# A one-core decoder kernel: the layer norms' statistics, transposes and evacuations rearranged by token halves

## What is computed

```python
for i in range(DEPTH):                      # DEPTH = 4
    kind, j = i % N_MIXERS, i // N_MIXERS   # fox, s5, pool, fox
    ...                                     # m = the mixer of h
    h = layer_norm(DN_ALPHA * h + m, ln_g[i, 0], ln_b[i, 0])
    h = layer_norm(DN_ALPHA * h + swiglu(h, ffn_w1[i], ffn_w3[i], ffn_w2[i]), ln_g[i, 1], ln_b[i, 1])

def layer_norm(h, g, b):
    mu = jnp.mean(h32, axis=-1, keepdims=True)
    var = jnp.mean(jnp.square(h32 - mu), axis=-1, keepdims=True)
    return ((h32 - mu) * lax.rsqrt(var + LN_EPS) * g + b).astype(h.dtype)
```

## Time and profile before

| | |
|---|---|
| median of the three runs | 1341.6 us (1338.08 to 1341.9) |
| the profiled execution, its own time | 1344.52 us |
| its span, first to last instruction | 1342.4 us |
| PE busy | 1247.0 us (93%) |
| DVE busy | 858.6 us (64%) |
| ACT busy | 606.3 us (45%) |
| granted TensorE clock, mean | 0.936 of 2.4 GHz |

### The profile page before, as it was taken

One profiled execution on the slowest core, in us unless ns is written; L12 is line 12 of the kernel. 1 busy time (PEld: TensorE's weight loads), 2 busy tenths in 40 slices (PEclk: granted clock), 3 DMA queues, 4 the chain that ended last, 5 costly groups with the idle time before them and its releaser, 6 DMA issues.

```text
span 1342.4 us, 20829 instructions
## 1 busy us (share of the span) xinstructions
PE 1247.0 (93%) x8432; PEld 1114.0 (83%) x8432; DVE 858.6 (64%) x1291; ACT 606.3 (45%) x944; POOL 160.2 (12%) x206
## 2 busy tenths in 40 slices
PE   5998899989989998999997789999989988999996
PEld 3886799989978766999996769999968976999996
DVE  5775879999575445655557866555567765655556
ACT  4465454444443224444444445444454653544442
POOL 2530008930090000000000000000002000000000
PEclk9997899989986778999998899999999988999998
DMA  9442356445585332665562536655535322566651
GB/s 356 157 150 78 110 189 204 142 154 188 162 187 164 129 111 95 225 198 188 188 189 98 170 110 196 218 184 188 186 127 188 118 88 94 189 220 188 187 184 69
DMA packets 63377, 220.35 MB, mean 164 GB/s; under 512 B 7985, under 2 KB 9777, under 8 KB 62513
## 3 DMA queue, kind: packets, MB, share of 16 engines
q1 hardware_dynamic: 56914, 202.50, 46.4%
q0 software_dynamic: 5504, 14.95, 3.8%
q10 hardware_dynamic: 864, 1.57, 0.4%
HBM read 210.34 MB, written 7.60 MB: 162 GB/s over the span
## 4 chain that ended last, share of the span: by engine, by line
PE 77%; DVE 15%; issue 3%; ACT 2%; DMA 1%; SPq 0%; DVEq 0%; ACTq 0%
PE bank L1249 15%; PE bank L1251 14%; PE bank L1250 14%; PE bank L1260 8%; PE bank L1262 8%; PE bank L1264 8%; DVE wlo L750 3%; PE bank L1274 2%; PE bank L1493 2%; DVE xlo L817 1%; DVE stats L763 1%; DVE slot L762 1%; PE bank L1424 1%; PE bank L1437 1%; ACT whi L462 1%
## 5 line engine op out<-in xcount | busy, mean ns | idle before, releaser
L750 DVE TENSOR_TENSOR wlo<-raw,whi 128x1024 fp32r<-128x1024 f32 x370 | 460.0, 1247 | 111.5 <-ACT whi L462 111.3
L1249 PE MATMUL bank<-xhi,whi 128*128 128x256 f32 x1728 | 498.7, 289 | 14.9 <-DVE xlo L817 10.1
L1250 PE MATMUL bank<-xlo,whi 128*128 128x256 f32 x1728 | 493.9, 286 | 0.0
L1251 PE MATMUL bank<-xhi,wlo 128*128 128x256 f32 x1728 | 493.7, 286 | 0.0
L462 ACT ACTIVATE whi<-raw 128x1024 fp32r<-128x1024 f32 x370 | 387.8, 1053 | 143.4 <-PE bank L1264 128.9
L1249 PEld LDWEIGHTS bank<-xhi,whi 128*128 128x128 f32 x1728 | 336.3, 195 | 24.2 <-DVE wlo L750 13.7
L1250 PEld LDWEIGHTS bank<-xlo,whi 128*128 128x128 f32 x1728 | 336.9, 195 | 2.8
L1251 PEld LDWEIGHTS bank<-xhi,wlo 128*128 128x128 f32 x1728 | 336.5, 195 | 0.0
L854 DVE TENSOR_TENSOR hval<-bank,silu 128x256 f32<-128x256 f32 x88 | 37.3, 424 | 231.0 <-PE bank L1251 231.0
L510 ACT ACTIVATE hhi<-hval 128x256 fp32r<-128x256 f32 x84 | 35.1, 418 | 194.3 <-DVE hval L854 194.3
L1260 PE MATMUL bank<-whi,hhi 128*128 128x512 f32 x304 | 95.3, 395 | 1.8 <-DVE wlo L750 1.8
(11 more groups left out here) (289 smaller groups left out, 1483.2 us busy)
## 6 DMA issues: line engine op xcount, KB each, us to landing
raw<-in_w SPq DMA_DIRECT2D x370, 512.0 KB, 3.9
slot<-in_ln_row POOLq DMA_DIRECT2D x16, 512.0 KB, 5.7
toep<-slot POOLq DMA_DIRECT2D x8, 512.0 KB, 15.3
toepA<-toep SPq DMA_DIRECT2D x2, 1024.0 KB, 7.4
BT<-toep SPq DMA_DIRECT2D x2, 1024.0 KB, 4.9
x_tm<-in_x SPq DMA_DIRECT2D x1, 1024.0 KB, 5.0
slot<-in_s_B SPq DMA_DIRECT2D x1, 1024.0 KB, 10.9
slot<-in_s_C SPq DMA_DIRECT2D x1, 1024.0 KB, 14.1
```

The source lines that it names most:

```text
L750: V.tensor_tensor(wlo[:, c % SPL, :], raw[:, c % RAW, :], whi[:, c % SPL, :].bitcast(F32), ALU.subtract).then_inc(w_lo, 1)
L1249: mm(dst, wh, bhi[:, kc, :], start=(i == 0), stop=False)
L1250: mm(dst, wh, blo[:, kc, :], start=False, stop=False)
L1251: ins = mm(dst, wl, bhi[:, kc, :], start=False, stop=(i == len(chunks) - 1))
```

## The change

The change is in the norms and at their edges.

1. **First half's statistics.** The two residual additions of token half 0 also write their row sums (`accum_out=sums`); a 128x1 instruction makes the negative mean `nmean`; ACT squares `res + nmean` over all 1024 columns with a row sum (`ssq`) and takes the square root of that. The two `bn_stats` and the `bn_aggr` of half 0 are gone. Half 1 keeps them.
2. **Transposes to separate banks.** Half 0 goes to banks 0 and 1 (four chunks each), half 1 to banks 4 to 7 (two chunks each). Every pair of transposes signals.
3. **Evacuation half by half.** Each 128x256 scale-and-shift becomes two of 128x128, one for each half: of half 0, pairs 0 and 1 by ACT, 2 and 3 by DVE; of half 1, pairs 0 and 2 by DVE, 1 and 3 by ACT. `xhi` of pair 0 is made in two halves. The second half's norm on DVE is issued in two pieces of 512 columns.
4. **Weight tiles.** Tile `first` is split before the norm (in the tails of `ffn`, `fox` and `poolmix`). In the norm only `first + 1` is split: by ACT behind the norming of half 0, by DVE at the very end. Before, DVE split `first` in front of `xlo` of pair 0 and the tiles up to `ahead` in front of `xlo` of pairs 2 and 3.
5. **End of a sublayer.** In `tm_end` the first of the three tiles is finished on bank 3 before bank 2 is complete.

```diff
@@ residual, DVE
-                step(V.scalar_tensor_tensor(res[:, m, cols], x_tm[:, m, cols], ALPHA, src, ALU.mult, ALU.add))
-                return V.bn_stats(stats[:, m, j, :], res[:, m, cols])
+                if m == 0:
+                    mark(V.scalar_tensor_tensor(res[:, m, cols], x_tm[:, m, cols], ALPHA, src, ALU.mult, ALU.add, accum_out=sums[:, j:j + 1]))
+                else:
+                    step(V.scalar_tensor_tensor(res[:, m, cols], x_tm[:, m, cols], ALPHA, src, ALU.mult, ALU.add))
+
+            def measure(j):
+
+                mark(V.bn_stats(stats[:, j, :], res[:, 1, j * HALF:(j + 1) * HALF]))
@@ ln, DVE
+                    summed(0, 0)
+                    summed(0, 1)
+                    marked()
+                    V.tensor_scalar(nmean[:, :], sums[:, 0:1], sums[:, 1:2], -1.0 / D, ALU.add, ALU.mult).then_inc(mean_ready, 1)
+                    summed(1, 0)
+                    if glu is None:
+                        measure(0)
+                    if n < n_ln - 1:
+                        mean_rstd(n, 0)
+                        dve.wait_ge(mean_ready, n + 1)
+                        V.tensor_scalar(nmr[:, :], nmean[:, :], rstd[:, 0, :], None, ALU.mult).then_inc(rstd_ready, 1)
+                    summed(1, 1)
+                    if glu is not None:
+                        measure(0)
+                    measure(1)
+                    marked()
+                    V.bn_aggr(mv[:, :], stats[:, :, :]).then_inc(var_ready, 1)
...
+                    value(2, 0)
+                    dve.wait_ge(var_ready, n + 1)
+                    mean_rstd(n, 1)
+                    for j in range(2):
+                        cols = slice(j * HALF, (j + 1) * HALF)
+                        V.tensor_scalar(res[:, 1, cols], res[:, 1, cols], mv[:, 0:1], rstd[:, 1, :], ALU.subtract, ALU.mult).then_inc(xn_ready[1], 1)
...
+                value(3, 0)
+                value(0, 1)
+                x_lo(0)
+                value(2, 1)
+                x_lo(1)
+                x_lo(2)
+                x_lo(3)
+                lo_to(ahead if n < 0 else first + 1)
@@ ln, ACT
+                    act.wait_ge(mean_ready, n + 1)
+                    step(nc.scalar.activation(slot[4][:, 0:D], res[:, 0, :], ACT.Square, bias=nmean[:, :], accum_out=ssq[:, :]))
+                    nc.scalar.activation(std[:, 0, :], ssq[:, :], ACT.Sqrt, scale=1.0 / D, bias=cst[:, C_EPS:C_EPS + 1]).then_inc(std_ready, 1)
...
+                value(0, 0)
+                value(1, 0)
+                act.wait_ge(xval0_act, 2 * (n + 1) + 1)
+                high0(0)
+                act.wait_ge(xval1_dve, 2 * (n + 1) + 1)
+                high0(1).then_inc(xhi_ready, 1)
+                value(1, 1)
+                high(1)
+                high(2)
+                value(3, 1)
+                high(3)
@@ tails of ffn (ACT; DVE the same with lo_to), fox, poolmix
                 nxt[0] = T0 + T_FFN
+                hi_to(T0 + T_FFN)
...
-                for c in range(KC - 2):
+                for c in range(KC - 1):
                     hi_to(T0 + KC + 2 * PAIRS + c + 2)
@@ tm_end, PE
-                for i in range(3):
-                    ins = all3(i, 2)
-                ins.then_inc(sub_done, 1)
-                for i in range(3):
-                    used(all3(i, 3))
+                all3(0, 2)
+                used(all3(0, 3))
+                all3(1, 2)
+                all3(2, 2).then_inc(sub_done, 1)
+                used(all3(1, 3))
+                used(all3(2, 3))
@@ lnT, PE
+                        ins = nc.tensor.transpose(xn_at(m, 2 * b + q), src[:, m, (2 * b + q) * P:(2 * b + q + 1) * P], ident)
+                        ins.then_inc(xnT_ready, 1)
```

More of the change, by code:

```diff
@@ new lines, in ln, with value @@
+                else:
+                    hi_to(ahead)
+                def value(b, m):
+                    act.wait_ge(xnT_ready, 8 * (n + 1) + 4 * m + (2 * (b // 2) + 2 if m == 0 else b + 1))
+                    for q in range(2):
+                        k, cols = 2 * b + q, slice(q * SEQ + m * P, q * SEQ + (m + 1) * P)
+                        if n < 0:
+                            ins = nc.scalar.copy(xval[:, b, cols], xn_at(m, k))
+                        else:
+                            ins = nc.scalar.activation(xval[:, b, cols], xn_at(m, k), ACT.Identity,
+                                                       scale=ln_col[:, 0, n, k:k + 1], bias=ln_col[:, 1, n, k:k + 1])
+                    ins.then_inc(xval0_act if m == 0 else xval1_act, 1)
@@ L885, in ffn @@
                 nxt[0] = T0 + T_FFN
+                lo_to(T0 + T_FFN)
             def fox(l, f):
```

150 lines of the change are left out of this document (73 added, 77 removed).

## The result

The changed kernel took 1346.45 us (median of 20 runs, 1339.99 to 1353.86), the kernel before 1339.93 in the runs beside it (20, 1333.98 to 1344.66). The ratio is 1.0052, 95% interval 1.0034 to 1.0071: some 6.5 us slower, where +2.6 was forecast. The time is inside the range of 1339 to 1349, but outside the forecast's own 1341 to 1346. The sign was right, the size was less than half. The difference passes the 4 us that the forecast set as its bound, so what came is the case "slower", to which it had given 0.28, and not "within", which had 0.62. The absolute time looks nearer (1344.1 forecast, 1346.45 measured) than the difference does, because the kernel before ran 1.7 us faster beside it (1339.93) than in the three runs that the forecast started from (1341.6); that is luck. (1341.6 and 2.6 are 1344.2, not the 1344.1 of the forecast.)

A forecast was written before the change was run, and what follows sets the result against it. PE's products set the time, except in short stretches where PE waits for DVE. Terms 1.8 + 0.7 − 2.0 + 2.0 + 0.1 = +2.6 us on the median 1341.6 gave 1344.1; range 1339 to 1349, the forecast's own 1341 to 1346.

The forecast's parts named there:

- the case "slower": Whole kernel: slower by more than 4 us (0.3%), the difference a measurement can hardly tell from none; chance 0.28.
- The statistics are not on the path: Inner norms: the root is ready 0.9 us before DVE's reciprocal, so statistics work taken off DVE saves nothing.
- tm_end costs only the 0.1 counted: Sublayer ends: the new product order, completing bank 2 three products later, adds only norm 7's +0.1 us.
- Rival 3: Norms: first-half statistics do leave the path, each norm up to 0.7 us shorter; 2.6 − 4.9 = −2.3 in all; chance 0.08.
- The price of 128 columns: Norm evacuations: a 128-column scale-and-shift out of PSUM takes 0.41 us on DVE, 0.44 on ACT.
- The dear and the cheap rival: Evacuations: 128 columns cost 0.54 us, total +9.6, chance 0.22; or 0.29 us, total −4.5, chance 0.10.
- Norms 3 and 5: +0.9 each: DVE, owing tile first + 2, ends these norms 0.95 us later and the mixers follow: +1.8 us together.
- norm 1's mixer: S5 mixer behind norm 1: same DVE delay as norms 3 and 5, a little shorter: +0.7 us.
- Start: the hold takes it up: 0: Attention start: DVE comes 1.35 us later, but a 3.60 us hold until POOL's copy ends absorbs it: 0.
- Norm 2: Behind the gated product: squares after the table load (+1.36), bn_stats (+0.6) and an evacuation delay the second half: +2.0 us.
- Norms 0, 4, 6: In front of FFNs: earlier xlo shortens the first tile from 5.88 to 5.20 us: −0.7 each, −2.0 together.
- Rival 4, the clock: PE clock: one or two more first tiles at 1.2 GHz add 2.9 us (1347.0), fewer gain as much; chance 0.12.

The follow-up runs named there:

- b_stats: Kernel before with only the first half's new statistics (sums with the addition, squares on ACT) in norms 0 to 6: 1334.22 us, ratio 0.9957.
- a_tmend: Changed kernel with the last six products of each tm_end in the old order (bank 2, then bank 3): 1342.45 us, ratio 1.0026.
- a_bn_all: Changed kernel with the first half's statistics back on DVE as before, in norms 0 to 6: 1347.8 us, ratio 1.0068.
- b_evac: Kernel before with only the half-wise transposes to separate banks, second-half norming in two pieces and half-wise evacuations: 1343.58 us, ratio 1.0048.
- a_poolhi: Changed kernel with ACT splitting pooling tile T0 + 2 ahead of its wait for DVE's memset: ratio 1.0051, pooling stage 40.59 instead of 41.80 us.
- b_late: Kernel before with two unused 512-column bn_stats (1.22 us) added on DVE at the end of the start transposition: 1339.42 us, ratio 0.9999.
- a_bn_2: Changed kernel with the first half's statistics as before in norm 2 alone: 1340.42 us, ratio 1.0033.
- b_tiles: Kernel before with the whole weight-tile part of the change, in front of FFNs and mixers: 1343.35 us, ratio 1.0027.

## Why the prediction was right in sign and short in size

**The statistics are not on the path: right, and for the reason given.** The forecast's words "the order of the products fixes it" are what b_stats and a_tmend show. With the old order the moved statistics shorten hole 3 by 0.55 us (six holes by 3.6); the new order makes bank 2 complete 0.70 us later and takes that back. So "tm_end costs only the 0.1 counted" holds only for the pair of edits together: taken by itself the order costs 4.4 us in the holes. The prediction counted the pair as next to nothing, which a_bn_all bears out to 0.07 us, but a reader should know that it was a gain and a loss, not two zeros. Rival 3 with its -4.9 was near the right size for the case that did not occur. Right too is the tile `first` ahead of the norm: DVE's idle time before the first addition falls from 1.52 to 0.39 us, by its 1.13, and the addition still finds its bank not ready.

**The price of 128 columns: right.** A pair on DVE takes 0.73, four take 1.36; on ACT four take 1.48, as 0.44 for the first and 0.35 for each further one have it (1.49). PE starts 0.27 later (0.26). The dear and the cheap rival both fall. The page "VectorE: DVE Perf Modes" of the Trainium skill, section on the TRN2 errata, gives an estimate of 0.26 us for such an instruction by its `120 + FD` cycles; here a further one adds 0.32 (0.63 for two, from a pair's 0.73 to the 1.36 of four), so one alone is 0.41, the value taken, and the trace is dearer than the page. Its advice on tiles of 512 elements agrees in sign: b_evac is slower.

**"Norms 3 and 5: +0.9 each" was the term that failed most.** The step reads "DVE is 0.95 later, and the mixer with it", and priced the owed tile by its 1.13 us alone. In norm 3 it left out where ACT's half of that tile stands: behind `wait_ge(pads_zero)`, so behind DVE's memset, which itself stands behind DVE's last tile. Hole and pooling stage are 2.33 us longer together (49.57 against 47.24), and a_poolhi puts 1.21 of that on the memset. The other 1.12 is the forecast's 0.95. Norm 5 cost 1.16 at DVE's gate, norm 1's mixer 1.32 (21.87 against 20.55) where +0.7 stood. Together these three are 4.8 where the sum has 2.5. For norm 3 that is PE's own lateness; for 1 and 5 it is that of ACT and DVE, and that PE pays all of it is assumed, as in the forecast.

**"Start: the hold takes it up: 0" was wrong.** The instruction is held for 3.6 us wherever DVE stands, so the hold has no slack to give; b_late and the changed kernel both show DVE as late behind as ahead of it, 1.1 to 1.3 us. What reaches PE is some 0.7 us by the means of the first `olo` (77.2 in eight kernels with a delayed start, 76.5 in the four with none), not resolved from its spread.

**Norm 2: right in size, wrong in one term.** +2.10 for the hole, +2.0 forecast. The two `bn_stats` ("+0.6") cost nothing, since DVE waits behind them for the transposes at the low clock anyway (a_bn_2); that evacuation makes the other 0.83. The squares are 1.27 (1.36 forecast), as the rows on ACT show:

```profile
522.75 1.28 ACT L490 ACT_TABLE_LOAD   x1
524.05 1.15 ACT L492 ACTIVATE slot<-slot,nmean 128x1024 f32<-128x1024 f32 x1
```

**Norms 0, 4, 6: the mechanism right, -0.7 each too much.** Between the first and the second tile's first product lie 5.34 us behind norm 6, where it was 5.88 and the forecast 5.20. But the granted clock comes back to 1.00 only some 6.3 us behind PE's start, in both kernels. A wait that is saved while PE runs at the lower level is then worth only the products that pass in it, at the upper level's price: two or three products of 0.12, not 0.54 us. (Behind norm 0 the clock came back 3.2 us after PE's start in the changed kernel and 6.1 before; the kernels of either kind have both, 5.8 in a_bn_2 and 3.2 in b_late, so the difference is not put down to the change.) Timelines of PE behind norm 6, first products of the two tiles:

```profile
1146.92 0.55 PE L1326 MATMUL bank<-xhi,whi 128*128 128x256 f32 x1 [1.13 <-DVE xlo L859]
...
1152.26 0.41 PE L1326 MATMUL bank<-xhi,whi 128*128 128x256 f32 x1
```

At the 31st product, when both run at the full clock, 0.35 of the 0.54 us is left. Behind norm 4, where the clock came back early in both (3.6 and 2.9 us), the third tile's first product is only 0.13 sooner, and the second tile waits 0.16 for its `wlo`, the last in DVE's queue. With holes of norms 4 and 6 0.17 and 0.06 longer this gives -0.8 at most for the three and not -2.0; the three FFN stages, each 0.5 to 0.6 shorter on the mean of all profiles with the new tile order, allow -1.5.

**The sum mended.** Start 0.7, norm 1 1.3, norm 2 2.1, norm 3 2.3, norm 5 1.2, norms 0, 4, 6 between -0.8 and -1.5: 6.1 to 6.8 us, with 6.5 measured (4.6 to 9.5 by the interval). That it closes so well is in part luck: only norms 2 and 3, 4.4 us, are read on PE to a tenth.

**By parts instead of places** the ratios of the single edits say: the evacuations in halves +0.48% (b_evac), the tiles +0.27% (b_tiles), the order of the products +0.26% (changed less a_tmend), the statistics -0.43% (b_stats). Together that is +0.58%, with 0.52 measured, and intervals of some 0.2 to either side of each. By the whole time the evacuations are the dearest part; 3.6 of their 6.4 us are found in the holes.

**Rival 4, the clock, is not excluded as a part.** The 20 runs of the changed kernel had a mean granted clock of 0.942; those of the kernel before beside the other kernels had 0.943 to 0.944 (of those beside the changed kernel none is on record). At the 1.3 us for each 0.001 that the changed kernel's own runs show, that would be some 2 to 3 us. Longer holes can themselves lower the mean clock, and nothing here parts the two.

## What to carry to other kernels

When work that was done ahead is left for later, look up on every engine where the later place stands: a tile of 1.1 us that one engine owes cost twice that, because its other half was queued behind a wait that had never mattered. Two edits that cancel look like one that does nothing, so try the parts alone: in the holes the statistics here were a gain that a reordering of products, made in the same change, undid. And where the clock is low when a wait is saved, count what a saved wait gives in products, not in microseconds.

## What the runs showed of the hardware beyond that

- DVE's accumulator read takes 0.08 us and no room in the queue: the next addition starts at the same time (720.46, both rows above), 0.61 behind the first. ACT's takes 0.18, and the next instruction starts 0.09 behind the read's start (row 66.24, next 66.33, before).
- A DVE instruction that starts beside POOL's copy into `qa` is held for 3.50 to 3.62 us in 12 of the 14 profiles, whichever instruction it is. In the other two it is a weight tile's split, which takes 4.59 and 4.50 us instead of 1.22: the hold adds some 3.3 us to a long instruction as to a short one.
- The time follows the mean granted clock even where the kernel is the same: in 20 runs of the changed kernel clocks of 0.937 to 0.948 go with 1353.9 down to 1340.0 us, about 1.3 us for each 0.001.
